# Four weight chunks of the layer-1 conditioning computed beside the GQA output projection instead of the compressed-key stage, and the seven half-size products of an FFN block in another order

## The reference

```python
# conditioning of each layer: six vectors of 1024 per stream
ada = jax.nn.silu(c) @ w_ada + b_ada          # shift1, scale1, gate1, shift2, scale2, gate2

# hybrid layer, compressed keys: rope, then blocks of 32 keys, and a small MLP on them
blk = t[:, idx] + pe[None, None, :, None, :]
kcmp = jax.nn.silu(blk @ w1) @ w2

# second model, a layer
h = h + gate1 * (mixer(norm_modulate(h, g1, shift1, scale1)) @ w_out)
u = norm_modulate(h, g2, shift2, scale2) @ w_up       # then conv, silu gate, w_down, * gate2
```

## Time and profile before

| what | value |
|---|---|
| median of three runs | 2296.41 us |
| profiled execution, device time | 2294.28 us |
| its span in the trace | 2292.5 us |
| PE busy | 2067.7 us (90%) |
| DVE busy | 1050.1 us (46%) |
| ACT busy | 548.7 us (24%) |
| mean granted TensorE clock | 0.95 of full |
| read from HBM | 354.84 MB |

### The profile page before, as it was taken

The page is one execution under the profiler, slowest core; times in us unless marked ns, Lnnn a source line. Parts: engine busy times, 40 slices in busy tenths (PEclk is TensorE's granted clock), DMA queues, the critical chain, the costliest instruction groups (busy, mean ns, idle before and its releaser), DMA issues.

```text
span 2292.5 us, 27822 instructions
## 1 busy us (share of the span) xinstructions
PE 2067.7 (90%) x10216; PEld 1449.6 (63%) x10216; DVE 1050.1 (46%) x2090; ACT 548.7 (24%) x1095; POOL 60.9 (3%) x69
## 2 busy tenths in 40 slices
PE   6999897888978999988978979999999688999997
PEld 4888685756864555545435458888444344678886
DVE  3456655435722222233666167777687312523311
ACT  3333200024021111122146023333000112524410
POOL 0000000000000000000000001110000010000000
PEclk9999998689988999999989989999999898999999
DMA  9444565130464999940000112223574011034451
GB/s 383 165 181 168 202 248 230 37 165 1 184 261 175 426 425 421 421 188 0 1 37 1 55 54 74 91 91 124 216 269 180 0 40 56 1 110 148 158 200 44
DMA packets 39081, 357.13 MB, mean 156 GB/s; under 512 B 4295, under 2 KB 8526, under 8 KB 9934
## 3 DMA queue, kind: packets, MB, share of 16 engines
q1 hardware_dynamic: 38990, 355.91, 39.6%
HBM read 354.84 MB, written 1.05 MB: 155 GB/s over the span
## 4 chain that ended last, share of the span: by engine, by line
PE 80%; DVE 6%; ACT 4%; PEld 3%; issue 3%; DMA 2%; DVEq 1%; PEldq 1%; SPq 0%; ACTq 0%
PE bank L636 43%; PE bank L1290 12%; PE bank L1097 6%; PEld bank L636 3%; PE bank L1083 3%; PE bank L1119 3%; PE bank L739 2%; DMA ring<-in_ada 2%; PE bank L662 1%; PE bank L1262 1%; ACT ring L1397 1%; DVE ring L1873 1%; ACT ring L1406 1%; DVE rstd L1805 1%; ACT hn L1369 1%
## 5 line engine op out<-in xcount | busy, mean ns | idle before, releaser
L636 PE MATMUL bank<-arena,ring 128*128 128x256 f32 (+4 forms) x1760 | 520.2, 456 | 39.8 <-issue 13.6
L636 PE MATMUL bank<-hn,ring 128*128 128x256 f32 (+1 forms) x2080 | 521.4, 411 | 14.1 <-ACT hn L1369 9.7
L636 PEld LDWEIGHTS bank<-hn,ring 128*128 128x128 f32 x2080 | 400.2, 193 | 123.5 <-issue 67.7
L636 PEld LDWEIGHTS bank<-arena,ring 128*128 128x128 f32 (+2 forms) x1760 | 334.1, 201 | 223.2 <-issue 165.5
L1290 PE MATMUL bank<-hn,ring 128*128 128x256 f32 x704 | 161.0, 382 | 6.2 <-ACT hn L1369 6.2
L1290 PEld LDWEIGHTS bank<-hn,ring 128*128 128x128 f32 x704 | 134.6, 191 | 25.6 <-issue 7.0
L1785 DVE SCALAR_TENSOR_TENSOR bank<-ring,c_rows 128x1024 f32<-128x1024 f32 x96 | 118.2, 1231 | 35.9 <-DMA ring<-in_ada 30.7
L1290 PE MATMUL bank<-ring 128*128 128x256 f32 x528 | 124.0, 385 | 5.9 <-DVEq L2505 5.9
L1785 DVE SCALAR_TENSOR_TENSOR ring<-ring,c_rows 128x1024 f32<-128x1024 f32 x96 | 117.2, 1221 | 0.0
L1858 DVE SCALAR_TENSOR_TENSOR resid<-bank,ada,resid 128x256 f32 x56 | 25.6, 482 | 198.9 <-PE bank L636 198.4
L1290 PEld LDWEIGHTS bank<-ring 128*128 128x128 f32 x528 | 102.2, 194 | 20.9 <-issue 6.6
(11 more groups left out here) (376 smaller groups left out, 2185.0 us busy)
## 6 DMA issues: line engine op xcount, KB each, us to landing
ring<-in_ada SPq DMA_DIRECT2D x28, 2048.0 KB, 10.1
ring<-in_up SPq DMA_DIRECT2D x44, 1024.0 KB, 4.8
ring<-in_egu SPq DMA_DIRECT2D x20, 2048.0 KB, 11.1
ring<-in_edn SPq DMA_DIRECT2D x39, 1024.0 KB, 9.6
ring<-in_down SPq DMA_DIRECT2D x16, 1408.0 KB, 9.7
arena<-in_egu SPq DMA_DIRECT2D x10, 2048.0 KB, 11.0
hn<-in_egu SPq DMA_DIRECT2D x9, 2048.0 KB, 10.9
ring<-in_adat SPq DMA_DIRECT2D x8, 2048.0 KB, 12.3
```

What stands on the lines that cost most here:

```text
L636: last = mm(out, lhs(i), rhs(i), start=i == 0, stop=i == k - 1)
```

## The change

Chunks 4 to 7 leave the compressed-key stage. The NSA output projection now takes chunks 4, 5, 8 and 9 (before: 8 to 11), and the GQA output projection takes 6, 7, 10 and 11 (before: none), a quarter of the four beside each pair of blocks: half a chunk before each block's gated add. In the FFN up-projection the product that uses `up_t3` comes before the one that uses `up_t2`; `up_t2` is computed from `up_t3`, so the activation sums come in the order t3, t2, t1, t4 (before: t3, t1, t2, t4), and PE waits for each only before its own product. DVE's first addition of a step waits for three products instead of two.

```diff
@@ SP's queue
-            stream(1, [("cw1", 1, at(0)), ("kv", 2, at(0)), ("kv", 3, at(1)), ("ada2", 4, at(4)), ("ada2", 5, at(5)),
-                       ("cw1", 0, at(1)), ("ada2", 4, at(6)), ("ada2", 5, at(7))])
+            stream(1, [("cw1", 1, at(0)), ("kv", 2, at(0)), ("kv", 3, at(1)), ("cw1", 0, at(1))])
             stream(4, [("q", 2, c1)])
-            stream(1, [("nga", 1, at(0)), ("ada2", 0, at(8)), ("ada2", 3, at(9)), ("nga", 2, at(1)), ("nga", 1, at(2)),
-                       ("ada2", 0, at(10)), ("nga", 2, at(3)), ("ada2", 3, at(11))])
+            stream(1, [("nga", 1, at(0)), ("ada2", 0, at(4)), ("ada2", 3, at(5)), ("nga", 2, at(1)), ("nga", 1, at(2)),
+                       ("ada2", 0, at(8)), ("nga", 2, at(3)), ("ada2", 3, at(9))])
...
-                    stream(2, [("gqao", 1, c2(0)), ("gqao", 3, c2(1))])
+                    stream(1, [("gqao", 1, at(0)), ("gqao", 3, at(1))])
+                    sp.wait_ge(phase, 3 * (GQA_QUERIES + 1))
+                    stream(1, [("ada2", 5, at(6)), ("ada2", 4, at(7)), ("gqao", 1, at(2)), ("ada2", 5, at(10)),
+                               ("gqao", 3, at(3)), ("ada2", 4, at(11))])
@@ PE, up_seven
                     pe.wait_ge(s["up_S"], i * 2 + (q + 1))
+                    pe.wait_ge(s["up_T"], 1)
+                    pe.wait_ge(s["up_added"], i * 14 + (7 * q + 7))
+                    product(2, sums[:, 2], lambda k: up_t3[:, k, :])
                     pe.wait_ge(s["up_T"], 2)
-                    pe.wait_ge(s["up_added"], i * 14 + (7 * q + 6))
                     product(1, sums[:, 1], lambda k: up_t2[:, k, :])
                     pe.wait_ge(s["up_T"], 3)
-                    pe.wait_ge(s["up_added"], i * 14 + (7 * q + 7))
-                    product(2, sums[:, 2], lambda k: up_t3[:, k, :])
                     product(3, sums[:, 0], lambda k: up_t1[:, k, :])
@@ DVE
+            def out_ada(i, m):
+
+                x, late = m // 2, m % 2
+                ada_turned(5 - x, None if late else i * 16 + 16 * nth["ada2", 6 + x], 1, i * 16 + (24 + 4 * x), x,
+                           range(2 * late, 2 * late + 2), late == 1, 4)
...
             end_phase()
-            for x in range(2):
-                ada_turned(4 + x, 16 * nth["ada2", 4 + x], 1, 16 + 4 * x, x, range(4), True, 6)
...
             ve.drain().then_inc(s["kv_ready"], 1)
-            for x in range(2):
-                ada_turned(4 + x, 16 * nth["ada2", 6 + x], 1, 24 + 4 * x, x, range(4), True, 5)
...
-            gated_out(False, (0, 3), (nth["ada2", 8], nth["ada2", 9]), 8)
+            gated_out(False, (0, 3), (nth["ada2", 4], nth["ada2", 5]), 4, 16)
...
-                    gemm(2, 4, T2, 16, 1)
+                    gemm(2, 4, T2, 16, 1, out_ada)
@@ DVE, up_second and up_outputs
-                    ve.wait_ge(s["up_p"], j * 7 + 2)
+                    ve.wait_ge(s["up_p"], j * 7 + 3)
...
-                    ve.wait_ge(s["up_p"], j * 7 + 3)
                     up_add(u3, u2, c)
@@ DVE, the sums of activations
                     V.tensor_tensor(up_t3, hn[:, 4:8, T:T2], hn[:, 0:4, T:T2], ALU.subtract)
-                    ve.drain()
+                    ve.drain().then_inc(s["up_T"], 1)
+                    V.tensor_tensor(up_t2, up_t3, hn[:, 0:4, 0:T], ALU.add)
+                    ve.drain().then_inc(s["up_T"], 1)
                     V.tensor_tensor(up_t1, hn[:, 0:4, T:T2], hn[:, 0:4, 0:T], ALU.subtract)
                     ve.drain().then_inc(s["up_T"], 1)
-                    V.tensor_tensor(up_t2, hn[:, 4:8, T:T2], up_t1, ALU.subtract)
-                    ve.drain().then_inc(s["up_T"], 2)
```

More of the change, by code:

```diff
@@ L954, in _ @@
             taken(1, 0, 1, 2, 3)
-            taken(2, 4, 5)
             pe.wait_ge(s["hid_silu"], 1)
@@ L1813, in norm, with gated_out @@
                 norms[0] += 1
-            def gated_out(first, ada_slots, taken, chunk):
+            def gated_out(first, ada_slots, taken, chunk, stride):
                 with ve.Fori(0, 2) as i:
@@ L1820, in gated_out @@
                         sl = ada_slots[m // 2]
-                        ada_turned(sl, i * 16 + 16 * taken[m // 2] if m % 2 == 0 else None, 1, i * 8 + (chunk + m // 2) * 4,
+                        ada_turned(sl, i * 16 + 16 * taken[m // 2] if m % 2 == 0 else None, 1, i * stride + (chunk + m // 2) * 4,
                                    m // 2, range(2) if m % 2 == 0 else range(2, 4), m % 2 == 1, 6)
@@ L2058, in _ @@
             end_phase()
-            gated_out(True, (1, 4), (nth["ada2", 0], nth["ada2", 1]), 0)
+            gated_out(True, (1, 4), (nth["ada2", 0], nth["ada2", 1]), 0, 8)
             end_phase()
-            for x in range(2):
-                ada_turned(4 + x, 16 * nth["ada2", 4 + x], 1, 16 + 4 * x, x, range(4), True, 6)
             ve.wait_ge(s["kv_mm"], 1)
```

## The result

The changed kernel takes **2282.12 us** (median of 4 runs, 2281.31 to 2282.81), the kernel before, beside it, 2296.75 us. The ratio is 0.9938, with a 95% interval of 0.9926 to 0.9950: 14.6 us or 0.6% less, and the interval leaves out a ratio of 1. Its profiled execution took 2281.93 us with a span of 2280.1; that of before had 2292.5, so between the two traces 12.4 us are to be explained. The page says "PE 84%" in the chain of waits, where it said 80%, and PE's busy time is 2065.8 us: PE does the same work with fewer holes.

What follows compares the result with a forecast made beforehand. PE was taken to bound the kernel (80% of the chain of waits), DVE counting only where PE stands still for it. Gains of 7.8 + 2.7 + 2.65 = 13.15 us off the 2296.4 us median gave 2283.2 us, range 2275 to 2291.

Steps and rivals of the forecast that it cites:

- the side that had 88%: Whole kernel: faster by more than 0.2% (4.6 us), against 8% for within that and 4% for slower.
- Part 1: Compressed-key stage: chunks 4 and 5 leave its front; PE goes on 7.8 us earlier, copies at 2.4 GHz save 2.7 us.
- The narrow matmuls: 128 matmuls of the compressed-key MLP, expected at 1.2 GHz again, 27.5 us as before: gain 0.
- the end of 3: Upper end of the narrow matmuls' gain: 3 us, if the clock falls only once they run.
- the rival of a full clock throughout: The narrow matmuls stay at 2.4 GHz, 13.8 us instead of 27.5: kernel at 2269.5 us; chance 5%.
- Parts 2 and 3: Chunks 6 and 7 leave the MLP's shadow; the NSA output projection only changes chunk numbers: 0 us each.
- Part 4: GQA output projection takes chunks 6, 7, 10, 11; first update 5.7 us late, caught up by the last; cost 0.
- The rival of a projection that takes it back: First landing so late that DVE bounds the GQA output projection: 9 us left, kernel at 2292 us; chance 4%.
- Part 5: Up-projection: new product order lets PE go on 2.65 us earlier at the start; DVE's later first addition costs 0.
- POOL, up to 0.8 us given back: Up-projection: the first weight sum, 1 us later, mostly misses POOL's work, which gives back up to 0.8 us.
- The slower rival: Later first addition makes DVE bound the up-projection: 1.0 us in each of 21 `up_second` steps, 2304 us; chance 4%.
- The sum, 13.15 us: Whole kernel: total forecast gain, 7.8 + 2.7 + 2.65 us.

Runs made afterwards that it cites:

- the first fill: Kernel before with 21 extra matmuls of ones on PE between the rotation and the copies of the compressed-key stage: 2296.56 us, ratio 0.9999.
- the third group: Last of three groups of follow-up kernels, each run beside the kernel before on one chip; that kernel's median there was 2296.72 us.

## Why the prediction was right

It gave 2283.2 us, in a range of 2275 to 2291; 2282.1 came out, on the side that had 88%.

- **Part 1, 7.8 and 2.7 us: right.** The hole and the copies went as forecast; 10.4 us against 10.5. The unsure term was the clock, and the first fill shows that it was the idle time that took it: with PE at work the copies ran at full clock in the kernel before too.
- **The narrow matmuls, 0 us: right**, 27.51 us again. Their price was no law of the stage, though. With no hole ahead they gave 5.0 us, more than the end of 3 that I had set for a clock that falls once they run, and the rival of a full clock throughout did not come even then. The Trainium skill (TensorE: Matmul & The Clock Gate, The HAM clock gate) has the throttled state as the default that sustained matmul work releases. Its rule holds for the wide form here (0.50, then 1.00) and fails for the narrow one, which went from 1.00 to 0.50 at work without a gap.
- **Parts 2 and 3, 0 us: right**, and for chunks 6 and 7 shown by putting them back.
- **Part 4, 0 us: right**, with sizes a little off: the first landing took 8.9 us instead of 7.8, the blocks 6.28 us instead of 6.33. The first update was 6.6 us late instead of 5.7, and 0.1 us of lag was left at the last one. The rival of a projection that takes it back falls; doubling the work is what it takes.
- **Part 5, 2.65 us: right**, 2.63 and 2.64 in two pairs of traces. That the later first addition costs nothing was right, **but its reason was wrong**. I wrote that DVE has 3.2 us a step to give, and looked for the harm in the next step's weight sums. The path is shorter: first addition, four sums, second addition, and PE's seventh product in the same step. The kernel before had 0.4 to 0.9 us of slack on it, the changed one has 0.1 to 0.9, and one product more costs 22 us. The slower rival named the right place and put its threshold more than 2 us too far out. It was much nearer than the 4% it got.
- **POOL, up to 0.8 us given back: right in one step of two, and it counted for more than I made of it.** A weight sum still meets POOL in every second step (20 of L2422 take 1.05 us on the mean, 0.69 alone and 1.42 beside POOL), where before one did in nearly each. DVE works 9 us less over the 22 steps, 0.4 us a step. I named this as one more argument against the rival. It decided: the delay of 1.0 to 1.1 us was larger than the slack that the kernel before had, and nothing was lost because the sums got shorter and the landing waits went. I had counted on neither with a number, so that the steps stayed at 12.1 us was in part luck.
- **The sum, 13.15 us**, is 13.0 in the traces and 14.6 in the medians. I had subtracted it from the median of three runs; from the profiled execution it would have given 2281.1, and the measured 2282.1 lies between the two, 1.1 us from either or less. The sum by the traces is what bears the prediction out. That the final number is so close is partly luck, since the medians moved by 1.6 us more than the traces let one explain.

## What to carry to other kernels

The slack of an engine over a step says little about a wait. Follow the queue behind the waiting instruction up to the one that another engine needs, and count the time to that one; then move the wait once more on the chip and see at what distance it bites. Work that waits for nothing belongs beside the longest gapless stretch of the other engine, and its price there is the period of a block, with the first landing to be caught up. And a gain in one stage is only had once the next place where the clock can fall has been passed: look at the granted clock there before blaming the edit, and take the lead over the other trace at several places, ahead of the edit too.

## What was not expected of the hardware

- Work without a gap did not always hold the full clock: 128 matmuls of 30 columns, back to back, went from 1.00 to 0.50 some 5.6 us after they began, and 64 of 256 columns went from 0.50 to 1.00 after some 5.7 us. Whether the columns or the weight loads beside them make the difference isn't shown. The same product takes 27.5, 22.5, 16.8 or 14.0 us, by its form and by what PE did ahead of it.
- Behind one hole of 2.46 us, at the same place of the same code, the half clock lasted 3.4 us in one kernel and 16 in another; why isn't shown. A kernel whose earlier part was 3.9 us shorter ended no sooner. With the hole filled the clock stayed at 1.00 through that stretch in all three kernels where it was tried.
- How far executions of one kernel lie apart goes with the clock. Of the 18 runs of the kernel before in the third group the three slowest (2298.94 to 2301.09 us) have a mean of 0.946 or 0.947, the three fastest (2294.67 to 2295.64) 0.950.
- DVE and POOL: a sum of 128x512 takes 0.69 us alone and 1.42 beside POOL's product of 1.27, in the kernel before up to 1.76.
